# A two-layer retention and sparse-attention decoder trunk in fp32r on one Trainium2 core: the last three chunks of each FFN down-projection walked output tile by output tile

## The reference

```python
def swiglu_ffn(x, norm_g, w_gu, w_down):
    h = rmsnorm(x, norm_g) @ w_gu          # 1024 -> 2 * 2816
    a, b = jnp.split(h, 2, axis=-1)
    return (jax.nn.silu(a) * b) @ w_down   # 2816 -> 1024

for layer in range(DEPTH):                 # DEPTH = 2
    x = x + 0.5 * swiglu_ffn(x, ffn1_norm[layer], ffn1_w_gu[layer], ffn1_w_down[layer])
    xn = rmsnorm(x, mix_norm[layer])
    if layer % N_MIXERS == 0:
        m = retention(xn, ret_w_in[j], ret_w_out[j])
    else:
        m = nsa(xn, nsa_w_in[j], nsa_w_out[j], ...)
    x = x + m
    x = x + 0.5 * swiglu_ffn(x, ffn2_norm[layer], ffn2_w_gu[layer], ffn2_w_down[layer])
```

## Time and profile before

| | |
|---|---|
| time, median of 3 runs | 2365.38 us (2361.45, 2365.38, 2367.03) |
| span of the profiled execution | 2360.2 us |
| PE busy | 2286.3 us, 97% of the span |
| POOL, DVE, ACT busy | 1064.1, 1043.0 and 840.6 us |
| weight chunks | 364 of 512 KB, median 3.2 us from issue to landing |
| mean granted TensorE clock | 0.982 of full speed |

### The profile page before, as it was taken

How to read it: one execution, slowest core, us unless ns; L and a number is a source line. 1 busy time by engine, 2 the same in 40 slices (tenths; PEclk the granted TensorE clock), 3 DMA queues, 4 the chain that set the end, 5 groups by cost and what they waited for, 6 DMA issues and landing times.

```text
span 2360.2 us, 30137 instructions
## 1 busy us (share of the span) xinstructions
PE 2286.3 (97%) x10390; PEld 1856.6 (79%) x10390; DVE 1043.0 (44%) x1767; ACT 840.6 (36%) x1267; POOL 1064.1 (45%) x699
## 2 busy tenths in 40 slices
PE   8999999999999899999999999998888889999999
PEld 6888887888888688888788888876677767888887
DVE  5434204566664744330244340078868863443301
ACT  5333213222122433331343331243367764333311
POOL 5444445444444544444454444464145455444442
PEclk9999999999999999999999999999988889999999
DMA  4222223222222132222232222132100012322221
GB/s 156 98 97 93 94 98 112 84 89 71 89 80 90 54 106 98 98 92 95 80 107 96 93 96 98 71 131 90 44 20 19 18 46 72 111 94 98 98 94 57
DMA packets 57780, 202.20 MB, mean 86 GB/s; under 512 B 6859, under 2 KB 7243, under 8 KB 57596
## 3 DMA queue, kind: packets, MB, share of 16 engines
q1 hardware_dynamic: 57724, 201.46, 24.8%
HBM read 199.29 MB, written 2.14 MB: 85 GB/s over the span
## 4 chain that ended last, share of the span: by engine, by line
PE 82%; DVE 10%; issue 4%; ACT 2%; POOL 1%; DMA 0%; DVEq 0%; SPq 0%; ACTq 0%; POOLq 0%
PE ps L711 17%; PE ps L713 17%; PE ps L712 17%; PE ps L739 7%; PE ps L741 7%; PE ps L740 7%; DVE xl L1091 2%; PE ps L729 2%; PE ps L731 2%; PE ps L730 2%; DVE std L1303 1%; PE ps L968 1%; PE ps L953 1%; DVE x L1102 1%; DVE kh L1314 1%
## 5 line engine op out<-in xcount | busy, mean ns | idle before, releaser
L366 POOL TENSOR_TENSOR wl<-raw,wh 128x1024 fp32r<-128x1024 f32 x364 | 879.3, 2418 | 1070.6 <-ACT wh L473 1070.6
L473 ACT ACTIVATE wh<-raw 128x1024 fp32r<-128x1024 f32 x364 | 385.4, 1062 | 1288.2 <-PE ps L713 808.0
L711 PE MATMUL ps<-xh,wh 128*128 128x512 f32 x1792 | 707.6, 395 | 12.8 <-DVE xl L1091 11.4
L712 PE MATMUL ps<-xl,wh 128*128 128x512 f32 x1792 | 698.5, 390 | 0.0
L713 PE MATMUL ps<-xh,wl 128*128 128x512 f32 x1792 | 698.5, 390 | 0.0
L711 PEld LDWEIGHTS ps<-xh,wh 128*128 128x128 f32 x1792 | 337.0, 188 | 98.8 <-DVE xl L1091 15.5
L712 PEld LDWEIGHTS ps<-xl,wh 128*128 128x128 f32 x1792 | 337.1, 188 | 71.1 <-issue 2.9
L713 PEld LDWEIGHTS ps<-xh,wl 128*128 128x128 f32 x1792 | 337.0, 188 | 70.9
L739 PE MATMUL ps<-uh,wh 128*128 (+1 forms) x672 | 266.4, 396 | 0.0
L740 PE MATMUL ps<-ul,wh 128*128 (+1 forms) x672 | 266.4, 396 | 0.0
L741 PE MATMUL ps<-uh,wl 128*128 (+1 forms) x672 | 266.4, 396 | 0.0
(11 more groups left out here) (229 smaller groups left out, 2788.9 us busy)
## 6 DMA issues: line engine op xcount, KB each, us to landing
raw<-stream SPq DMA_DIRECT2D x364, 512.0 KB, 3.2
tn<-rel_rows SPq DMA_DIRECT2D x16, 256.0 KB, 3.2
xin<-x_in SPq DMA_DIRECT2D x4, 512.0 KB, 5.4
out<-xin SPq DMA_DIRECT2D x8, 256.0 KB, 2.5
dec<-c_dec SPq DMA_DIRECT2D x1, 1024.0 KB, 5.5
rotq<-c_rot SPq DMA_DIRECT2D x1, 512.0 KB, 3.1
vf<-gate_w SPq DMA_DIRECT2D x1, 192.0 KB, 2.1
csq<-c_sq SPq DMA_DIRECT2D x1, 128.5 KB, 2.0
```

The source lines that it names most:

```text
L366: nc.gpsimd.tensor_tensor(wl[:, slot, :], raw[:, slot, :], wh[:, slot, :].bitcast(F32), ALU.subtract).then_inc(chunk_lo, 1)
L473: nc.scalar.activation(wh[:, slot, :], raw[:, slot, :], ACT.Copy).then_inc(chunk_hi, 1)
L711: mm(o, w_h, hi, start=k == 0, stop=False)
L712: mm(o, w_h, lo, start=False, stop=False)
```

## The change

The last three chunks of each down-projection (f = 19, 20, 21) are no longer walked one after another with all eight d in each. PE waits until all three are staged and then walks d outside and f inside: nine matmuls in a row to bank d, which is then complete. `down_mm` counts up after each d < 7. All three chunks are released (`chunk_mm`) only in the last tile, d = 7, one after each chunk's third matmul there. ACT and POOL are reordered to fit: before `norm_later` and `sum_squares` only the next stage's first chunk is staged, the second to the fourth behind them. The chunks before f = 19 keep their form (four loop iterations and two chunks written out in place of five and one).

```diff
+LASTS = 3
...
-            lows(ahead, C_RET + ahead)
+            lows(ahead, C_RET + SLOTS - LASTS)
             sum_squares(1)
-            low(chunk(C_RET + ahead))
-
-            lows(C_RET + 4, C_RET + 16)
+            lows(C_RET + SLOTS - LASTS, C_RET + 16)
...
-            for m, c0 in ((2, C_FFN[1]), (3, C_FFN[2]), (4, C_NSA)):
-                lows(at, c0 + ahead)
+            for m, c0, early in ((2, C_FFN[1], ahead), (3, C_FFN[2], SLOTS - LASTS), (4, C_NSA, SLOTS - LASTS)):
+                lows(at, c0 + early)
                 sum_squares(m)
-                at = c0 + ahead
+                at = c0 + early
             lows(at, C_NOUT)
...
-                    wide(c0 + UP, FT - 1)
+                    wide(c0 + UP, FT - LASTS)
                     norm_later(following)
-                    after(c0 + UP + FT - 1)
+                    after(c0 + UP + FT - LASTS, LASTS)
...
-                n = (FT - 2) // 4
+                n = (FT - 1 - LASTS) // 4
...
-                for f in range(1 + 4 * n, FT):
+                for f in range(1 + 4 * n, FT - LASTS):
                     pe.wait_ge(u_ready, u0 + f + 1)
-                    wide_chunk(chunk(cd + f), uh[:, f, :], ul[:, f, :], range(KT), False, f == FT - 1)
+                    wide_chunk(chunk(cd + f), uh[:, f, :], ul[:, f, :], range(KT), False, False)
+                pe.wait_ge(u_ready, u0 + FT)
+                pe.wait_ge(chunk_lo, cd + FT)
+                for d in range(KT):
+                    for f in range(FT - LASTS, FT):
+                        c, slot, turn = chunk(cd + f)
+                        w_h, w_l = wh[:, slot, d * P:(d + 1) * P], wl[:, slot, d * P:(d + 1) * P]
+                        mm(ps[:, d, :], w_h, uh[:, f, :], start=False, stop=False)
+                        mm(ps[:, d, :], w_h, ul[:, f, :], start=False, stop=False)
+                        last = mm(ps[:, d, :], w_l, uh[:, f, :], start=False, stop=f == FT - 1)
+                        if d == KT - 1:
+                            last.then_inc(chunk_mm, 1)
+                        elif f == FT - 1:
+                            last.then_inc(down_mm, 1)
```

## The result

The changed kernel takes 2359.27 us (median of 14 runs, 2356.19 to 2364.04), the kernel before 2364.07 us (median of 14, 2361.31 to 2367.03). The ratio is 0.998, with a 95% interval of 0.9973 to 0.9986: 4.8 us or 0.2% faster.

A forecast was written before the change was run, and what follows sets the result against it. PE, busy for 97% of the span, was taken to bound the kernel. Three junctions each gain 2.53 and lose 1.06 us, 4.4 us in all: 2365.4 - 4.4 = 2361.0 us; range 2356.5 to 2366.0 us.

The forecast's parts named there:

- The wait for `xl` goes entirely: Between the next stage's first matmul and the norm's matmul (a junction), PE's wait for DVE vanishes: 2.53 us gained each.
- The wait for `wl` that takes its place: At each junction's 25th matmul, PE waits for the next stage's second chunk from POOL: 1.06 us lost.
- The walk by tiles at nothing: In the down-projection, the same 72 matmuls in another order cost nothing; bounds -2.2 to +1.0 us.
- a 17% rival: Down walk at 0.2266 us a matmul, 2.2 us, giving 2358.8 us; 17% together with the refill in time.
- No wait ahead of the walk: Before f = 19, PE's earlier need of f = 21's `wl` costs nothing, with 1.9 us to spare.
- the tiles fit: During the walk, DVE's 1.81 us for each tile fit into the 2.11 us in which a bank completes.
- the third and fourth chunk are hidden: Behind the junction's second chunk, the next two chunks' `wl` cost PE no wait, 3.6 us to spare at the first.
- FFN 3 unchanged: After FFN 3's last matmul, PE's 32 transposes follow without a gap (3.65 us); nothing to gain.
- The refill is in time: In junctions, POOL readies the second chunk's `wl` in time, winning all 7.6 us: 2357.8 us; 17% together with faster walk.
- Only its name changes: In junctions, PE waits for `wl` as long as it did for `xl`; time stays at 2365.4 us; 13%.
- The slower rival: In the walk, each `xl` takes 1.98 us, tiles overrun 2.11 us, PE waits 4.5 us: 2371.2 us; 10%.

The follow-up runs named there:

- the two versions in which it does happen: Changed kernel with only the last two chunks by tiles, 2356.49 us; changed kernel with the second chunk staged ahead of the last tile, 2357.9 us.

## Why the prediction was right, point by point

*The time.* 2361.0 us were forecast and 2359.27 measured. Of the 1.7 us between them, 1.3 are the kernel before, whose median over 14 runs is 2364.07 and not 2365.38, and 0.4 are the gain itself, 4.8 in place of 4.4 us.

*The wait for `xl` goes entirely, 2.53 us a junction.* Right: no such wait is left in the three, and with the second chunk out of the way the 48 matmuls take 10.90 us, against the 10.88 worked out.

*The wait for `wl` that takes its place, 1.06 us.* Right in kind and place; it is 0.94 us, and that accounts for the 4.8 us where 4.4 was forecast. The 25th matmul came 0.76 us late, not 0.95, and the matmuls behind it lost 0.18 us more, not 0.11. The `wl` was ready 5.93 us after tile 7's `x`, not 6.13. I had taken over the 2.83 us of the earlier trace rows; this time POOL's add was held (1.55 us) and the `wl` was not (2.37 us). That is the order of events to which the lock rule of the Trainium skill (SBUF — State Buffer, "SBUF: two separate sides") had led. The trace agrees with it: DVE's last `xl` ends at 389.72, inside that add, and the add ends 1.15 us behind it. But the prediction had put the `wl` by this rule within 0.1 us of the row, and it came 0.2 us earlier. That this one `wl` alone is what PE waited for, two experiments show from both sides: staged earlier, the loss is gone; one add later, it grows by the add's time.

*The walk by tiles at nothing.* Right: 0.2343 us before and after. The rows of the gate product led to the right value, but as a reason they were worth less than I took them for. Their 0.231 us has another cause than the walk's 0.2343, since in the version with the last two chunks and the 96 bytes, where the walk goes at 0.2267, the same 22 steps still take 5.06 us, 0.230 each:

```profile
1646.83 0.40 PE L929 MATMUL ps<-xl,vst 128*48 128x512 f32 x1
...
1651.89 0.40 PE L930 MATMUL ps<-xh,vst 128*48 128x512 f32 x1
```

What the rows could not tell was why either walk is slower than 0.2266 us; I had put down the cause as not shown, and as part of a 17% rival. It has nothing to do with the order of the walk: it is where `uh` and `ul` start.

*No wait ahead of the walk; the tiles fit; the third and fourth chunk are hidden; FFN 3 unchanged.* All four are as the profile after shows: no wait at 370.20, 0.33 us of idle time on DVE ahead of the `x` shown, no other wait for `wl` in the junctions, and in FFN 3 the transposes follow without a gap (2349.77, again 3.65 us).

*The rivals.* "The refill is in time" did not happen in this change, and it would have been worth what I gave for it: the two versions in which it does happen measured 9.1 and 7.7 us below the kernel before, where 7.6 us were worked out (the interval of the first reaches down to 5.0 us, so its excess says nothing). "Only its name changes" needed 1.5 us of delay, and what one more add does (+2.4 us at least in each junction) shows how near that was: one instruction on POOL. The slower rival did not come; no `xl` in the walk shown took more than 1.2 us.

*The span.* Between the two profiled executions the span falls by 1.9 us only, not by 4.4. The windows say where the rest is: 0.53 us in the start of the program, and 438.54 - 436.26 = 2.28 us from NSA's norm to FFN 3, a stretch that the change doesn't touch, with a mean granted clock of 0.91 where it was 0.92. -4.77 + 0.53 + 2.28 = -1.96. Another trace tells more about the second: the version with 32 more bytes holds the whole change, and its same stretch is

```profile
1541.97:1978.28 436.31, 392.10 (x2098) 0.91 0.17 53
```

as short as before the change, 436.26 us. In the six traces with the same SBUF layout (this change, the kernel before, and four of the versions above), none of which edits this stretch, it goes from 436.26 to 441.03 us, and the first matmul of FFN 0 starts between 15.60 and 16.74 us. So both differences lie within what these stretches vary by, and nothing ties them to the change.

## What to carry to other kernels

Walk only as many last chunks by output tile as the consumer needs: each one more holds a buffer to the very end, and the refill behind it can become the next wait. What counts is the first use, so let a late tile be late where PE reaches it last, and give the engines' time to the chunk that it reaches first. And where one matmul form is a few per cent slower than another of the same shape, look at where its operands start in SBUF before anything is reordered: 96 unused bytes were worth 17.0 us here, the whole reordering 4.8.

## What was not expected of the hardware

*The start of a moving operand.* The down-projection's matmuls (weights 128x128, moving operand 128x512, both in fp32r) start every 0.2267 us where all moving operands start at a multiple of 128 bytes in the partition, every 0.2333 us where they start 64 bytes past one, every 0.2343 us 32 bytes past one, and every 0.2317 us where one operand in three is 32 past. Other offsets, types and sizes were not looked at, nor does any run tell whether the same holds for weights. An aligned moving operand is not enough everywhere: NSA's gate product moves `xh` and `xl`, which start at multiples of 128, and stays at 0.230 to 0.231 us in both layouts. Its weights are 48 columns wide, and why it is slower stays open.

*The clock behind a wait.* After a wait of 3.0 us for POOL the granted clock fell in two junctions of three, and matmuls started 0.42 us apart instead of 0.23. Two windows of the second junction with one more add (all engines; the clock is the third number from the right) show both levels, 0.50 (1.2 GHz) and 1.00 (2.4 GHz):

```profile
1180.00:1182.00 2.00, 2.00 (x6) 1.53 (x5) 0.00 (x0) 0.00 (x0) 2.00 (x2) 0.50 0.58 227
...
1184.00:1186.00 2.00, 2.00 (x11) 1.48 (x9) 0.00 (x0) 0.00 (x0) 0.00 (x0) 1.00 0.76 262
```

It cost 15.82 - 14.20 = 1.6 us in the second junction and about as much in the third, half of the wait itself once more. The waits of 0.6 us for `wl` in the changed kernel left the clock at 1.00 in all three junctions; the waits of 7 us in the version with the staging order alone took it down in all three (0.75 to 0.83). Why the first junction was spared the 3.0 us stays open.

*A DVE `xl` behind a POOL add.* The first `xl` of the changed walk has POOL idle beside it, the second starts inside an add:

```profile
375.23 0.74 DVE L1103 SCALAR_TENSOR_TENSOR xl<-x,gain,xh 128x512 fp32r<-128x512 f32 x1
377.33 1.18 DVE L1103 SCALAR_TENSOR_TENSOR xl<-x,gain,xh 128x512 fp32r<-128x512 f32 x1
376.67 1.29 POOL L385 TENSOR_TENSOR std<-sq 128x512 f32<-128x512 f32 x1 [2.67 <-ACT sq L483]
```

Alone it takes 0.74 us; the second ends 0.55 us after the add, and the one of 1.98 us in the earlier trace rows ended 0.55 us after the `wl` beside it. So the 1.81 us for each tile, from which the prediction explains the old loss, hold waits for POOL. By an estimate from these rows a tile without them would take DVE 0.61 + 0.74 = 1.35 us, no more than the 1.36 us in which PE uses one up. What the old junction would lose with the adds out of DVE's way was not run.
